# A transformer layer with two attention branches and 32 experts on one core: the latent heads' values computed by features for two heads at once, scores a step ahead, division and norm weight moved

## What is computed

```python
xn = rms_norm(h, attn_norm); proj = xn @ w_in                  # q_lat, kv_lat, k_pe, dq, dk, dv, gates
o_a = mla_branch(...)    # 8 latent heads: q,k of 96, v of 64; softmax over up to 256 keys, causal
o_b = diff_branch(...)   # 4 differential heads, v of 128; o[0] - lam*o[1], then
o_b = rms_norm(o_b, subln) * (1 - lambda_init)                 # norm over the 128 features of a head
merged = sigmoid(gate_a) * (o_a @ w_branch_mla) + sigmoid(gate_b) * (o_b @ w_branch_diff)
h = h + merged @ w_out
h = h + moe_ffn(rms_norm(h, ffn_norm))   # 32 experts, 4 per token, 1024 -> 2*1024 -> 1024
```

## Time and profile before

| | |
|---|---|
| median of 3 runs | 1113.33 us (1112.65 to 1113.94) |
| profiled execution | 1114.4 us, its span 1112.7 us |
| granted TensorE clock, mean | 0.994 of full speed |
| busy: TensorE, VectorE, ScalarE, GpSimd | 96%, 30%, 18%, 4% of the span |
| chain that ended last | TensorE 72%, DMA 25% |
| moved | 438.66 MB, mean 394 GB/s |

### The profile page before, as it was taken

The page is one execution under the profiler, slowest core; times in us unless marked ns, Lnnn a source line. Parts: engine busy times, 40 slices in busy tenths (PEclk is TensorE's granted clock), DMA queues, the critical chain, the costliest instruction groups (busy, mean ns, idle before and its releaser), DMA issues.

```text
span 1112.7 us, 12604 instructions
## 1 busy us (share of the span) xinstructions
PE 1066.4 (96%) x5154; PEld 499.8 (45%) x5154; DVE 333.8 (30%) x611; ACT 195.1 (18%) x337; POOL 43.3 (4%) x66
## 2 busy tenths in 40 slices
PE   9999999999999999999999898989898989898997
PEld 9887888633434343434343333333332424242432
DVE  5889667322212212121212121211121212120212
ACT  7677673400001000100000000000000000000000
POOL 1335020000000000000000000000000000000000
PEclk9999999999999999999999999999999999999999
DMA  9764359999999999999999999999999999999996
GB/s 362 303 222 147 134 206 425 376 429 426 429 427 428 429 426 429 432 432 432 431 432 431 434 431 431 431 430 434 431 432 431 432 434 431 431 432 431 426 423 260
DMA packets 27988, 438.66 MB, mean 394 GB/s; under 512 B 3248, under 2 KB 3504, under 8 KB 6704
## 3 DMA queue, kind: packets, MB, share of 16 engines
q1 hardware_dynamic: 27072, 431.46, 92.1%
q10 hardware_dynamic: 880, 6.69, 1.4%
HBM read 437.08 MB, written 1.05 MB: 394 GB/s over the span
## 4 chain that ended last, share of the span: by engine, by line
PE 72%; DMA 25%; ACT 1%; DVE 1%; issue 1%; SPq 0%; ACTq 0%
DMA ring<-in_expert_q 25%; PE bank L995 22%; PE bank L1021 19%; PE bank L530 10%; PE bank L963 5%; PE bank L926 5%; PE bank L517 3%; PE bank L845 2%; PE bank L604 2%; PE bank L569 1%; PE bank L653 0%; DVE ring_s L1484 0%; DMA g_col<-in_g_turned 0%; PE bank L961 0%; PE bank L641 0%
## 5 line engine op out<-in xcount | busy, mean ns | idle before, releaser
L995 PE MATMUL bank<-ring,feat_r 128*64 128x512 f32 x1504 | 335.6, 599 | 13.0 <-DMA ring<-in_expert_q 13.0
L995 PEld LDWEIGHTS bank<-ring,feat_r 128*64 128x64 f32 x1504 | 105.0, 138 | 233.4 <-issue 210.1
L1021 PE MATMUL bank<-ring,feat_r 128*64 128x512 f32 x768 | 173.5, 596 | 13.3 <-DMA ring<-in_expert_q 12.8
L1857 DVE TENSOR_SCALAR late_r<-bank 128x512 f32<-128x512 f32 x32 | 22.1, 692 | 422.9 <-PE bank L995 422.9
L995 PE MATMUL bank<-pool_r,feat_r 128*64 128x512 f32 x512 | 116.7, 602 | 11.3 <-DMA pool_r<-in_expert_q 11.2
L530 PE MATMUL bank<-ring_s,feat_s 128*128 128x512 f32 (+2 forms) x396 | 121.2, 387 | 0.2
L1021 PEld LDWEIGHTS bank<-ring,feat_r 128*64 128x64 f32 x768 | 53.8, 137 | 119.6 <-issue 112.2
L1428 ACT ACTIVATE late_r<-late_r 128x512 f32<-128x512 f32 x32 | 20.2, 630 | 469.9 <-DVE late_r L1857 469.9
L1881 DVE TENSOR_TENSOR acc_r<-bank,acc_r 128x512 f32<-128x512 f32 x64 | 44.3, 692 | 150.8 <-PE bank L963 150.8
L530 PEld LDWEIGHTS bank<-ring_s,feat_s 128*128 128x128 f32 x396 | 71.2, 188 | 13.6 <-issue 1.0
L530 PE MATMUL bank<-ring_s 128*128 128x512 f32 (+2 forms) x196 | 74.3, 379 | 0.0
(11 more groups left out here) (225 smaller groups left out, 684.4 us busy)
## 6 DMA issues: line engine op xcount, KB each, us to landing
ring<-in_expert_q SPq DMA_DIRECT2D x45, 4096.0 KB, 27.4
ring<-in_expert_q SPq DMA_DIRECT2D x41, 2048.0 KB, 21.0
pool_r<-in_expert_q SPq DMA_DIRECT2D x15, 4096.0 KB, 29.3
pool_r<-in_expert_q SPq DMA_DIRECT2D x16, 2048.0 KB, 20.5
ring<-in_head_w SPq DMA_DIRECT2D x23, 1024.0 KB, 5.0
ring<-in_expert_q SPq DMA_DIRECT2D x21, 1024.0 KB, 15.9
ring<-in_head_w SPq DMA_DIRECT2D x5, 768.0 KB, 13.0
qkT_r<-in_expert_q ACTq DMA_DIRECT2D x1, 2048.0 KB, 14.4
```

The lines of the kernel that those rows point to most:

```text
L995: mm = pe.matmul(b[e * SLOTS:(e + 1) * SLOTS, :], xT[:, k, e * SLOTS:(e + 1) * SLOTS], w[:, e, g, :], start=(late and k == 0), stop=(k == ...
L1021: mm = pe.matmul(bank[4 + h][e * SLOTS:(e + 1) * SLOTS, :], aT[k // 4][:, k % 4, e * SLOTS:(e + 1) * SLOTS], w[:, q, e, :], start=(k == 0) ...
L1857: ts(glu, bank[2 * f][:], LIMIT, None, ALU.min).then_inc(sem(f"glu_ready{f}"), 1)
```

## The change

Three things move together. The latent heads' values are formed for two heads side by side and by features: the 64 columns of `va` of a head are stationary, the turned probabilities move, the first head's result stands in PSUM rows 0 to 63 and the second's in rows 64 to 127 (`pair_values`), so that `o_aT` is already turned and the eight transposes go. The division can no longer be made on the result, so VectorE divides the probabilities in place before they are turned (`probs_scale`), and TensorE's `probs_turn` waits for that. Scores, mask, exponential and division of head s+1 run in step s. The norm of `o_b` moves from GpSimd to VectorE (`ob_scale`), and its weight becomes a column that ScalarE and VectorE apply while they copy the turned `o_b` (`sub_gain`). The square root and what follows it stand two steps later.

```diff
@@ SyncE
                 elif s_ == 0:
-                    sp.wait_ge(sem("valued"), HD + HA)
+                    sp.wait_ge(sem("valued"), HD + HA // 2)
                 elif s_ == 1:
                     sp.wait_ge(sem("qka_turned"), HA)
-                    sp.wait_ge(sem("o_turned"), 4)
+                    sp.wait_ge(sem("featT_ready"), 4)
@@ GpSimd
-            pool.wait_ge(sem("ob_norm_steps"), 2)
-            for m in range(NM):
...
-                pool.tensor_tensor(o_b[:, m], o_b[:, m], r, ALU.mult).then_inc(sem("ob_normed"), 1)
...
-                pool.tensor_tensor(o_b[:, m], o_b[:, m], g_sub.unsqueeze(1).broadcast_to([P, HD, DV]), ALU.mult)\
-                    .then_inc(sem("ob_ready"), 1)
@@ TensorE
+            def pair_values(i):
+
+                pe.wait_ge(sem("probsT_copied"), HD + 2 * i + 2)
+                if i >= 2:
+                    pe.wait_ge(sem("headed"), HD + i - 1)
+                b = bank[4 + i % 2]
+                for kt, c in ((0, slice(0, SEQ)), (1, slice(P, SEQ))):
+                    for e in range(2):
+                        mm = pe.matmul(b[e * VA:(e + 1) * VA, c], va[:, kt, 2 * i + e, :],
+                                       probsT[:, e, 0:2 * P] if kt == 0 else probsT[:, e, 2 * P:3 * P],
+                                       start=(kt == 0), stop=(kt == 1), skip_group_check=True)
+                mm.then_inc(sem("valued"), 1)
@@ TensorE, the loop
             for s in range(SUB, HEADS):
-                if s != SUB + 1:
+                if s == SUB:
                     scores(s)
+                if s < HEADS - 1:
+                    scores(s + 1)
                 if s == SUB:
-                    scores(s + 1)
...
                 if s == HEADS - 1:
                     o_b_turn(0)
                 gate_part(s, 0)
                 if s > SUB:
                     probs_turn(s - 1 - HD)
                 gate_part(s, 1, (0,) if s == HEADS - 1 else (0, 1))
-                if s > SUB:
-                    values(s - 1 - HD)
+                if s > SUB and (s - SUB) % 2 == 0:
+                    pair_values((s - SUB) // 2 - 1)
@@ TensorE, after the loop
-            pe.wait_ge(sem("headed"), HD + HA)
-            for m in range(NM):
-                for i in range(HD):
-                    mm = turn(bank[2 + m][:, i * P:(i + 1) * P],
-                              o_a[:, m, 2 * i:2 * i + 2, :].rearrange("p a b -> p (a b)"))
-                mm.then_inc(sem("o_turned"), 1)
+            pe.wait_ge(sem("headed"), HD + HA // 2)
@@ ScalarE, the loop
+                if s == SUB + 3:
+                    act.wait_ge(sem("gate_half"), 1)
+                    gate_copy(s // 4, 0)
+                if s == SUB:
                     exps(s)
+                else:
                     probsT_copy(t - 1)
...
+                exps(s + 1)
...
-                if s == SUB + 3:
+                if s == SUB + 5:
                     act.wait_ge(sem("ob_summed"), NM)
                     act.activation(ssq[:, 40:40 + 2 * HD], ssq[:, 40:40 + 2 * HD], ACT.Sqrt, bias=eps[:],
                                    scale=1.0 / DV).then_inc(sem("ob_norm_steps"), 1)
@@ VectorE
+            def probs_scale(s):
                 dve.wait_ge(sem("exped"), 2 * (s + 1))
                 link(dve.reciprocal(rsum[:, 2 * s:2 * s + 2], sums[:, 2 * s:2 * s + 2]))
...
+                for m in range(NM):
+                    c = slice(0, P) if m == 0 else slice(P, 3 * P)
+                    ts(scored[:, s % 4, c], scored[:, s % 4, c], rsum[:, 2 * s + m:2 * s + m + 1], None, ALU.mult)\
+                        .then_inc(sem("combined"), 1)
...
+            def ob_scale(m):
+                r = rstd[:, 40 + HD * m:40 + HD * (m + 1)].unsqueeze(2).broadcast_to([P, HD, DV])
+                tt(o_b[:, m], o_b[:, m], r, ALU.mult).then_inc(sem("ob_ready"), 1)
...
+                if s < SUB + HA - 1:
+                    probs_scale(s + 1)
...
+                elif s == SUB + 6:
                     dve.wait_ge(sem("ob_norm_steps"), 1)
...
+                    link(dve.reciprocal(rstd[:, 40:48], ssq[:, 40:48]))
+                    ob_scale(0)
+                if s > SUB and (s - SUB) % 2 == 0:
+                    pair_out((s - SUB) // 2 - 1)
```

More of the change, by code:

```diff
@@ L202, in build @@
         qlat, kvlat = v3(lat_r[:, 0:NM * Q_LORA], NM), v3(lat_r[:, NM * Q_LORA:], NM)
-        o_a = lat_r[:, 0:NM * WA].rearrange("p (m h d) -> p m h d", m=NM, h=HA)
+        o_aT = v3(lat_r[:, 0:NM * WA], HA // 2)
         qkd = qkd_r.rearrange("p (m h d) -> p m h d", m=NM, h=2 * SUB)
@@ L236, in build @@
         eps = sb("eps", 1)
-        g_col = sb("g_col", KD)
+        g_col = sb("g_col", KD + 1)
+        sub_gain = g_col[:, KD:KD + 1]
         ssq = sb("ssq", 64)
@@ L536, in split_part @@
                     mm.then_inc(sem("h_first"), 1)
+                return mm
             def split_product(banks, chunks):
@@ L768, in _ @@
             o_b_turn(1)
-            values(HD + HA - 1)
+            pair_values(HA // 2 - 1)
             for m in range(NM):
@@ L1679, in _, with oT_lo @@
                 dve.tensor_copy(qkaT[0:QK_A, 2 * i:2 * i + 2, :], v3(bank[p_][0:QK_A, :], 2)).then_inc(sem("qkaT_copied1"), 1)
-            ts(g_sub, g_sub, 1.0 - LAMBDA_INIT, None, ALU.mult).then_inc(sem("sub_gain_scaled"), 1)
-            def diff_piece(s):
+            ts(sub_gain, sub_gain, 1.0 - LAMBDA_INIT, None, ALU.mult).then_inc(sem("sub_gain_scaled"), 1)
+            def ob_scale(m):
+                r = rstd[:, 40 + HD * m:40 + HD * (m + 1)].unsqueeze(2).broadcast_to([P, HD, DV])
+                tt(o_b[:, m], o_b[:, m], r, ALU.mult).then_inc(sem("ob_ready"), 1)
+            def oT_lo(m):
+                dve.wait_ge(sem("featT_hi"), m + 1)
+                c = slice(m * P, (m + 1) * P)
+                stt(featT[1][:, 0:4, c], v3(bank[m][:], 4), sub_gain, featT[0][:, 0:4, c], ALU.mult, ALU.subtract)\
+                    .then_inc(sem("featT_ready"), 1)
+            for s in range(SUB, SUB + HA + 1):
+                if s == SUB:
+                    scale_mask(s)
+                if s < SUB + HA - 1:
+                    scale_mask(s + 1)
+                if s == SUB + HA - 1:
+                    ob_scale(1)
+                    oT_lo(0)
+                if s > SUB:
+                    split_lo(14 + (s - 1) // 2, ((s - 1) % 2,))
+                if s == SUB + HA:
+                    oT_lo(1)
+                if s == SUB:
+                    probs_scale(s)
+                if s < SUB + HA - 1:
+                    probs_scale(s + 1)
                 if s == SUB + 2:
@@ L1710, in gate @@
                     tt(g, bank[b0 + m][:], g, ALU.mult).then_inc(sem("branch_gated"), 1)
-            for m in range(NM):
-                turned_lo(2 + m, 4, m, 2 + m, 0)
+            for h in range(2):
+                dve.wait_ge(sem("featT_hi"), 3 + h)
+                k = slice(4 + 2 * h, 6 + 2 * h)
+                tt(featT[1][:, k, :], o_aT[:, 2 * h:2 * h + 2, :], featT[0][:, k, :], ALU.subtract)\
+                    .then_inc(sem("featT_ready"), 1)
             dve.wait_ge(sem("gates_ready"), NM)
```

95 lines of the change are left out of this document (40 added, 55 removed).

## The result

The changed kernel takes 1114.76 us (1112.83 to 1116.16, 22 runs) against 1113.33 us for the kernel before (1111.96 to 1114.58, 22 runs). The ratio is 1.0013, with a 95% interval of 1.0007 to 1.0019: 1.4 us slower, less than the 2.2 us of my bound, but more than this measurement is uncertain. I had forecast 1113.2, 0.1 us faster. The profiled execution took 1115.39 us, its span is 1113.7 us.

A forecast was written before the change was run, and what follows sets the result against it. The weights' stream bounds the kernel, its last hole dated by TensorE: the loop ends 0.16 us later, 0.80 us of transposes go, VectorE's chain takes most back; 0.1 us gained, 1113.2 us, range 1110.7 to 1115.8.

The forecast's parts named there:

- my bound: On the whole kernel's time: a change of less than 0.2% (2.2 us) cannot be told from none.
- The weights' stream: From the middle of the kernel to its end, this DMA stream sets the time; a pair of experts takes 58.28 us.
- its last hole: At 212 to 216 us the stream drops to 360 GB/s, as SyncE waits for slots that TensorE frees.
- The wait: At the head of step 15 TensorE's transposes of o_b idle 2.5 us behind VectorE's ob_scale.
- The halves run side by side: In pair_values a pair of heads costs 0.75 us; rival at 1.44, one half after the other, 12%.
- no drain: At ScalarE's table load before exps(15) none was forecast; rival with a drain of about 1.38 us: 1114.6, 4%.
- The late issue of slot 1: After the loop, SyncE issues slot 1 near 166 against 162.0, at no cost since transfers under way cover until 172.
- The sum: From o_b's transposes to the first branch product 5.2 us, where it was 5.67 before.
- this case as a rival: Behind the wait at o_b TensorE's clock falls to 1.2 GHz: +1.6 us, 1114.8; chance 11%.
- 5% together with the halves: Rival: the clock falls behind the wait and a pair's halves run one after the other, 1116.9; chance 5%.
- VectorE's chain: After the loop, VectorE's work towards the merged halves moves by +0.16 to 175.7, so TensorE, there at 174.8, waits.
- the 0.16 of the loop: At the loop's end, the first branch product starts at 155.5, 0.16 us later than before.

The follow-up runs named there:

- b_fill: The changed kernel with ten products of ones, results unused, on TensorE in place of the wait before o_b's turn: 1113.08 us, ratio to before 0.9999.
- Experiment 5: GpSimd's router product moved: ahead of its o_b work in the kernel before, ratio 1.0002; until the merged rows are turned in the changed kernel, 1.0008.
- a_ob_first: The changed kernel with ob_scale(0) one place earlier on VectorE, ahead of head 15's divisions: 1111.93 us, ratio to before 0.9985.
- e_ob_first_router_late: a_ob_first with GpSimd's product of the router's weights held until the merged rows are turned: 1111.08 us, ratio to before 0.9981.

## Why the prediction was wrong, step by step

**Right.** The weights' stream sets the end, and its last hole moves with TensorE: in the twelve traces the ratios follow the issue of slot 1's second lap, from 91.9 us (0.9981) to 95.9 (1.0013). The wait is where I put it, for the reason that I gave, 2.29 us against 2.5. The halves run side by side: 131.83 to 132.63 is 0.80 us for a pair, against 0.75, and far from 1.44. The table load brings no drain: it ends at 149.38 and the exponential starts at 149.40. So the row was right to decide over the drain of about 1.38 us that the Trainium skill has in ScalarE: Activation LUTs, section What ACT_TABLE_LOAD costs, which I had cited. The late issue of slot 1 is covered.

**The step that failed first: the wait was costed as its own length and nothing more.** The sum had 5.2 us from `o_b`'s turn to the first branch product. That is right only at 2.4 GHz: b_fill has 5.25 (151.07 to 156.32), the changed kernel 6.85 (152.05 to 158.90). I had this case as a rival, with its price right to the decimal (+1.6, measured 1.59), and gave it 11%, and 5% together with the halves. My own rows spoke louder than that: of eight waits of 2.62 to 2.64 us three were followed by the lower clock, and the new wait was of nearly that length. The forecast should have carried the rival at nearly three in eight. This term alone puts the time at 1114.8. That the measured 1114.76 is the rival's own number is luck in part: the three errors that follow, +0.36, +0.30 and -0.64, cancel.

**The step that was missing: +0.36 us ahead of the loop.** I took GpSimd's work on `o_b` away at no cost and looked only for who had waited for it. What stood behind it in GpSimd's list moved up as well, 39 us, to a place beside VectorE's `combine(2)`, which is on TensorE's path. Experiment 5 shows it.

**The step that erred to the other side: after the loop.** My sum had TensorE 0.80 us sooner at the merged rows for the eight turns and let VectorE's chain take back all but 0.26 of it (0.26, less the 0.16 of the loop, was my 0.1). The trace gives the full 0.90 us (20.09 to 19.19), since that chain came sooner as well: from the first branch product to the low parts of `o_aT` or `o_a` it was 9.38 us before (155.34 to 164.72) and is 8.05 after (158.90 to 166.95). I had read the chain's place from a trace in which a weight issue held ScalarE for 1.6 us. With such a delay put back, 0.56 of 0.90 us are lost again.

**A small one.** Without the clock the loop is 0.46 us longer (36.71 to 37.17), where I had 0.16. A pair of heads costs more than its own 0.80 us: from the last record of one gate product to the first of the next, a step with a pair takes 1.00 us longer than one without (131.50 to 133.20 against 127.73 to 128.43), against my 0.75. Two pairs stand ahead of step 14, and it begins 24.89 us behind the loop's start (120.14 to 145.03), where I had 24.61 (118.63 to 143.24). The 0.20 us beyond the 0.80 lie half ahead of the pair and half behind it, where TensorE goes from one form of the array to the other and back; that the switch is their cause is argued from the place. The page TensorEngine Tiling (Array Packing) of the Trainium skill, section Key Properties, says that changing the form drains the array; by this trace that is at most some 0.10 us each time, far from the price at which it would have decided.

Together: forecast -0.1; clock +1.59, start +0.36, loop +0.30 (0.46 against 0.16) and after the loop -0.64 (0.90 against 0.26) give +1.5, against +1.4 measured. What I can't account for is below the scatter. Not tried is why ScalarE's issue was long in the three kernels with the old loop (1.62, 1.33 and 1.16 us) and 0.36 in every one with the new.

## What to carry to other kernels

A wait has two prices, its length and what the clock may do behind it, so a forecast should carry both, the second with the share of such waits in the trace that a fall follows. Where TensorE would stand still for two microseconds or more, work that is of no use but keeps it busy can be worth more than it costs (b_fill), and moving one independent operation ahead of a late one on the engine that it waits for is better still (a_ob_first). When work is taken off an engine, look at what comes up behind it and beside whom it then runs, and not only at who waited for it. Before a freed microsecond is written off against a second chain, check that this chain's place in the trace is not itself the result of an accident that the change removes.

## What the runs showed of the hardware that I had not expected

- The clock fell behind both waits of 2.29 us: 0.59 and 0.57 of full speed in the 4 us behind them, with 1.59 us lost. It stayed at full speed after 1.20 us. Over the twelve traces it fell behind 51 of 95 waits of 2.62 to 2.65 us, behind none of 45 of 1.97 to 2.00, and once behind one of 1.57.
- The fall can come after the wait has ended. In single microseconds behind the end of equal waits in a_ob_first the clock reads 1.00, 0.58, 0.50, 0.50 (848.47), then 0.96, 0.50, 0.50, 0.50 (906.74), 0.84, 0.50, 0.50, 0.50 (965.02) and 0.71, 0.50, 0.50, 0.58 (1023.29): it falls some 0.25 us earlier from one wait to the next, though the waits are alike.
- VectorE and GpSimd slow each other. Two `combine` operations took 0.75 us alone, 1.28 with 0.73 us of overlap (105.39 to GpSimd's end at 95.94 + 10.18 = 106.12), and 1.64 with 1.36 us of overlap (106.54 to 107.90): 0.53 and 0.89 us more, some two thirds of the overlap. The other way round GpSimd's product for the router, 0.61 to 0.66 us in its two early places, took 1.73 us in e_ob_first_router_late (180.53), beside a VectorE pair that kept its usual 2.35 us.
- The Trainium skill, SBUF — State Buffer, section SBUF: two separate sides, has the shared port pair of these two engines as an exclusive lock for a whole instruction, with the loser fully blocked. By that the operations would be longer by all of the overlap, 2.1 us in the second case; the measured 1.64 decides, though that the two disturb each other at all is as the page says, and GpSimd's 1.73 us, 1.1 more with 1.24 us of overlap, comes near it.
- Issuing one and the same weight transfer on ScalarE's queue took 1.62, 1.33 and 1.16 us of the engine in the three kernels with the old loop and 0.36 in the nine with the new one. The cause is open.
